# Second feed-forward of a two-layer backbone on one core: order of activations, of loads and of the last accumulation steps

## The reference

```python
def conv_ffn(h, w_up, conv_w, conv_b, w_down):
    T = h.shape[1]
    u = h @ w_up                                   # 1024 x 1024 @ 1024 x 5632
    up = jnp.pad(u, ((0, 0), (CONV_W // 2, CONV_W // 2), (0, 0)))
    u = sum(up[:, j:j + T] * conv_w[j] for j in range(CONV_W)) + conv_b
    gate, val = jnp.split(u, 2, axis=-1)           # 2816 each
    return (jax.nn.silu(gate) * val) @ w_down      # 2816 x 1024
...
    f = conv_ffn(modulate(x, mod[3], mod[4]), w_up[l], conv_w[l], conv_b[l], w_down[l])
    x = layer_norm(DEEPNORM_ALPHA * x + mod[5] * f, ln2_g[l], ln2_b[l])
```

## Time and profile before

| | us |
|---|---|
| median of 3 runs | 3586.43 (3586.16 to 3586.73) |
| the profiled execution | 3590.86, its span 3589.1 |
| TensorE busy in the span | 3399.7 (95%) |
| VectorE, ScalarE, GpSimd busy | 1741.4, 1194.6, 1188.3 |
| blocks 6 to 21 (seven products) | from 2993.2 to 3316.2 |
| down projection | from 3316.5 to 3577.1 |

### The profile page before, as it was taken

How to read it: one execution, slowest core, us unless ns; L and a number is a source line. 1 busy time by engine, 2 the same in 40 slices (tenths; PEclk the granted TensorE clock), 3 DMA queues, 4 the chain that set the end, 5 groups by cost and what they waited for, 6 DMA issues and landing times.

```text
span 3589.1 us, 57973 instructions
## 1 busy us (share of the span) xinstructions
PE 3399.7 (95%) x24535; PEld 2796.5 (78%) x24535; DVE 1741.4 (49%) x2789; ACT 1194.6 (33%) x1747; POOL 1188.3 (33%) x526
## 2 busy tenths in 40 slices
PE   7999999988999999999999899999979999999998
PEld 6777778877868888888887677788867678777787
DVE  4333563056177344433435743364067676555564
ACT  4334564124233111111113333365134334444332
POOL 1221101302233333333333311201303447888442
PEclk9999999999999999999999899999999999999999
DMA  5111001352201111111111101000162132222543
GB/s 195 32 23 30 1 2 48 100 182 55 72 24 41 36 41 36 36 42 36 36 42 71 29 23 29 24 2 19 36 201 66 53 118 62 79 74 89 202 157 113
DMA packets 288117, 229.46 MB, mean 64 GB/s; under 512 B 47068, under 2 KB 257908, under 8 KB 287860
## 3 DMA queue, kind: packets, MB, share of 16 engines
q1 hardware_dynamic: 286704, 225.28, 20.4%
q10 hardware_dynamic: 1156, 0.48, 0.0%
HBM read 201.60 MB, written 24.12 MB: 63 GB/s over the span
## 4 chain that ended last, share of the span: by engine, by line
PE 78%; POOL 8%; DVE 8%; issue 3%; ACT 2%; DMA 1%; SPq 1%; ACTq 0%; DVEq 0%; POOLq 0%
PE psum L1341 49%; PE psum L1132 6%; PE psum L1895 6%; PE psum L1447 5%; POOL up_op L1065 4%; PE psum L1605 3%; PE psum L1141 2%; PE psum L1533 2%; PE psum L1369 1%; POOL up_sums L1079 1%; DVE c_x L2594 1%; PE psum L1564 1%; PE psum L1689 1%; PE psum L1267 1%; DVE h_lo L2370 1%
## 5 line engine op out<-in xcount | busy, mean ns | idle before, releaser
L1341 PE MATMUL psum<-h_hi,w_split 128*128 128x512 f32 (+1 forms) x4992 | 1185.9, 367 | 20.8 <-DVEq L767 6.2
L1029 POOL TENSOR_SCALAR w_split<-w_raw 128x1024 fp32r<-128x1024 f32 x142 | 399.1, 2811 | 2067.6 <-PE psum L1341 1328.5
L1341 PEld LDWEIGHTS psum<-h_hi,w_split 128*128 128x128 f32 x4992 | 847.6, 188 | 195.3 <-issue 26.0
L1341 PE MATMUL psum<-h_lo,w_split 128*128 128x512 f32 (+1 forms) x2496 | 650.2, 364 | 0.0
L1341 PEld LDWEIGHTS psum<-h_lo,w_split 128*128 128x128 f32 x2496 | 424.7, 188 | 78.5
L2774 DVE SCALAR_TENSOR_TENSOR f_t<-psum,vec,f_t 128x1023 f32<-128x1023 f32 x194 | 170.3, 915 | 393.4 <-ACT f_t L3502 391.6
L1031 POOL TENSOR_TENSOR w_split<-w_raw,w_split 128x1024 fp32r<-128x1024 f32 x142 | 349.1, 2459 | 11.8
L3502 ACT ACTIVATE f_t<-psum,vec 128x1280 f32<-128x1280 f32 (+1 forms) x53 | 73.1, 1380 | 531.1 <-PE psum L1341 518.0
L1341 PE MATMUL psum<-f_hi,w_split 128*128 128x512 f32 (+1 forms) x1056 | 239.7, 357 | 1.5 <-DVE f_t L2774 1.5
L1341 PEld LDWEIGHTS psum<-f_hi,w_split 128*128 128x128 f32 x1056 | 176.2, 188 | 36.2 <-issue 5.7
L2630 DVE SCALAR_TENSOR_TENSOR y_chan<-psum,mods,y_chan 128x1024 f32<-128x1024 f32 (+1 forms) x176 | 146.3, 877 | 97.7 <-PE psum L1341 97.5
(11 more groups left out here) (360 smaller groups left out, 5389.0 us busy)
## 6 DMA issues: line engine op xcount, KB each, us to landing
ada_late<-in_w_ada_dram SPq DMA_DIRECT2D x32, 1024.0 KB, 7.0
w_raw<-in_w_up_dram SPq DMA_DIRECT2D x56, 512.0 KB, 3.8
w_raw<-in_w_in_dram SPq DMA_DIRECT2D x42, 512.0 KB, 3.8
w_raw<-in_w_down_dram SPq DMA_DIRECT2D x40, 512.0 KB, 3.7
up_raw<-in_w_up_dram SPq DMA_DIRECT2D x32, 512.0 KB, 5.3
f_raw<-f_mid SPq DMA_DIRECT2D x44, 256.0 KB, 3.9
l_raw<-in_w_down_dram SPq DMA_DIRECT2D x17, 512.0 KB, 3.6
ada<-in_w_ada_dram SPq DMA_DIRECT2D x4, 2048.0 KB, 16.5
```

The source lines that it names most:

```text
L1029: pool.tensor_scalar(w_hi[:, n % 2], w_raw[:, n % 2], 1.0, None, ALU.mult).then_inc(s["w_hi_done"], 1)
L1341: last = pe.matmul(columns(key, t0, t0 + tn), weight, a[:, k, t0:t0 + tn], start=(k == order[0] and j == 0), stop=(closes and k == order[- ...
```

## The change

1. Blocks 3 to 5. ScalarE's `begin(3, 0)` and `silu(3)`, and VectorE's `conv(3, 0)`, stand ahead of the first differences (VectorE's also ahead of the wait for `r_stored`). SyncE issues the weights of block 4's gate half after the fourth of the eight residual stores instead of behind the eighth.
2. The four low halves `h_lo` that GpSimd made in round 0 go to VectorE (`last_low_differences`).
3. Seven-product rounds. On ScalarE `begin(f - 1, 1)` and `silu(f - 1)` stand ahead of high operand 4. On GpSimd sum 2 stands behind low 1; low halves 0 and 1 count on `raw_ready`, the other five on `op_ready`.
4. Hand-over to the down projection. The homes of `w2` 1 and 2 change places; loads, and the splits into them, wait for the last product that reads the home instead of for all products; the eight reads of `y_back` are spread over steps 5 to 8 of the loads and the residual is added after step 8 instead of after step 4; the order of `gate_weights`, `low_tokens`, `conv(21, 1)`, `high_weights` changes.
5. `LAST_STEPS` = 2 becomes (2, 4): in the second group the last four steps run tile by tile.

```diff
-LAST_STEPS = 2
+LAST_STEPS = (2, 4)
...
-        w2 = [(h_raw[:, :, LAT + P:T], h_lo[:, :, LAT:LAT + P], h_lo[:, :, LAT + P:T]), in_w(1, pair_at), in_w(2, ring_at)]
+        w2 = [(h_raw[:, :, LAT + P:T], h_lo[:, :, LAT:LAT + P], h_lo[:, :, LAT + P:T]), in_w(1, ring_at), in_w(2, pair_at)]
...
                 def load_down(n):
-                    if n == 1:
-                        sp.wait_ge(s["op_ready"], 7 * N_FAST)
-                    elif 2 <= n < N_W2:
-                        sp.wait_ge(s["prod_done"], 7 * N_FAST)
+                    if n == 2:
+                        sp.wait_ge(s["op_ready"], 5 * N_FAST)
+                        sp.wait_ge(s["raw_ready"], 2 * N_FAST)
+                    elif 1 <= n < N_W2:
+                        sp.wait_ge(s["prod_done"], 7 * (N_FAST - 1) + 4)
...
                     elif n < N_F2:
-                        sp.wait_ge(s["prod_done"], 7 * N_FAST)
+                        sp.wait_ge(s["prod_done"], 7 * (N_FAST - 1) + 5)
...
                             sp.dma_start(r_mid[k], y_chan[:, k, 0:LAT]).then_inc(s["r_stored"], 16)
+                            if k == 3:
+                                weights_up_to("up", l, 4, 0)
...
                 for i in range(N_FAST):
+                    if i == N_FAST - 1:
+                        load_f(0)
+                        load_f(1)
                     store(fast_f + i - 1)
...
-                load_f(0)
-                load_f(1)
-                load_down(1)
-                load_f(2)
-                load_down(2)
+                for n in range(1, N_W2):
+                    load_down(n)
+                    if n > 1:
+                        load_f(n)
                 sp.wait_ge(s["r_stored"], 2 * 16 * KT)
-                for m in range(KT):
-                    sp.dma_start(y_back[:, m, 0:LAT], r_mid[m]).then_inc(s["y_back"], 16)
...
+                for n in range(N_W2, 2 * FT):
+                    if n < N_W2 + 4:
+                        for m in (2 * (n - N_W2), 2 * (n - N_W2) + 1):
+                            sp.dma_start(y_back[:, m, 0:LAT], r_mid[m]).then_inc(s["y_back"], 16)
...
                     pool.tensor_tensor(one, a21, a22, ALU.add).then_inc(s["sum_done"], 1)
-                    low(0, a11)
+                    for j, whole in enumerate((a11, a12)):
+                        n = 7 * i + j
+                        pool.wait_ge(s["op_hi"], n + 1)
+                        pool.tensor_tensor(up_ops[n % 4][:, 1], whole, up_ops[n % 4][:, 0].bitcast(F32), ALU.subtract)\
+                            .then_inc(s["raw_ready"], 1)
                     pool.wait_ge(s["sum_done"], 4 * i + 1)
                     pool.tensor_tensor(two, one, a11, ALU.subtract).then_inc(s["sum_done"], 1)
-                    low(1, a12)
                     pool.wait_ge(s["sum_done"], 4 * i + 2)
                     low(2, two)
...
-                    if i == 0:
-                        pool.wait_ge(s["t_ready"], 12)
-                        for k in range(4):
-                            pool.wait_ge(s["t_split_hi"], 13 + k)
-                            pool.tensor_tensor(h_lo[:, k, HALF:LAT], t_one[:, k], h_hi[:, k, HALF:LAT].bitcast(F32), ALU.subtract)\
-                                .then_inc(s["t_ready"], 1)
...
-                    if n == 1:
-                        pool.wait_ge(s["prod_done"], 7 * N_FAST)
+                    if n in (1, 2, 4):
+                        pool.wait_ge(s["prod_done"], 7 * N_FAST - (n != 2))
...
-                        if k == 4:
+                        if k == 8:
                             old_sums(group)
...
+                def last_low_differences():
+
+                    for k in range(4):
+                        dve.wait_ge(s["t_split_hi"], 13 + k)
+                        say("t_ready", dve.tensor_tensor(h_lo[:, k, HALF:LAT], t_one[:, k], h_hi[:, k, HALF:LAT].bitcast(F32),
+                                                         ALU.subtract))
...
                     gated(2)
+                    conv(3, 0)
                     dve.wait_ge(s["r_stored"], 2 * 16 * KT)
                     differences(0)
-                    conv(3, 0)
                     conv(3, 1)
...
                             if n == 1 and i == N_FAST - 1:
                                 low_tokens(0)
                                 low_tokens(1)
-                        if i == N_FAST - 1:
-                            gate_weights(1)
+                                gate_weights(1)
                         conv(f, 0)
-                    conv(FT - 1, 1)
                     gate_weights(2)
                     low_tokens(2)
+                    conv(FT - 1, 1)
                     gated(FT - 1)
...
-                    high_differences(0)
                     begin(3, 0)
                     silu(3)
+                    high_differences(0)
                     begin(3, 1)
...
                         take(i, 0)
-                        ahead(1)
                         if i:
                             begin(f - 1, 1)
                             silu(f - 1)
+                        ahead(1)
                         ahead(2)
                         take(i, 1)
...
                     begin(FT - 1, 1)
+                    high_tokens(2)
                     silu(FT - 1)
+                    high_weights(2)
```

More of the change, by code:

```diff
@@ L1907, in down_by_token @@
                 for group in range(2):
-                    for k in range(FT - LAST_STEPS):
+                    for k in range(FT - LAST_STEPS[group]):
                         n = FT * group + k
@@ L1924, in down_by_token @@
                     for i in range(4):
-                        for k in range(FT - LAST_STEPS, FT):
+                        for k in range(FT - LAST_STEPS[group], FT):
                             last = part(FT * group + k, i, False, k == FT - 1)
@@ L2875, in two_phases @@
                     differences(3)
-                    for half in range(2):
-                        conv(5, half)
+                    conv(5, 0)
+                    last_low_differences()
+                    conv(5, 1)
                     gated(5)
@@ L3442, in phase_post @@
             def phase_post():
-                for n in range(2, 2 * FT):
+                for n in range(3, 2 * FT):
                     if n == FT + 3:
@@ L3587, in two_phases @@
                     high_differences(3)
+                    begin(5, 0)
                     for n in range(3):
-                        if n == 2:
-                            begin(5, 0)
                         high_operand(n)
```

34 lines of the change are left out of this document (17 added, 17 removed).

## The result

The changed kernel takes 3566.91 us (median of 4 runs, 3562.34 to 3573.13), the kernel before 3586.58 in its runs beside it (4 runs, 3586.16 to 3589.08). The ratio is 0.9945, with a 95% interval of 0.9928 to 0.9962: the interval leaves 1 out, so the changed kernel is faster, by 19.7 us. The forecast was 3566.6.

What follows compares the result with a forecast made beforehand. The prediction took the loop of GpSimd and ScalarE, 20.22 us a round, as the bound. Terms 8.0 + 3.3 + 5.2 + 1.0 + 2.3 + 0 = 19.8 us took 3586.4 to 3566.6; range 3559 to 3576.

Steps and rivals of the forecast that it cites:

- Part 1, 8.0: Blocks 3 to 5: 5.1 for the wait in front of block 4 plus 2.9 for the clock; bounds 5 and 8.1.
- what would be late "next": Block 4's weight tile: with its load issued between residual stores, GpSimd's split starts near 2930 and ends six us early.
- the head start: Round 0: four low halves, 5.1 us of GpSimd, go to VectorE; 3.3 us gained, bounds 0 and 5.1.
- The timetable: GpSimd's seven-product round rebuilt instruction by instruction: from 20.22 to about 19.85 us, 5.2 us over fourteen rounds.
- the slower rival: Rounds: late gate taps make GpSimd, ScalarE and VectorE wait in a loop; 22.3 us a round, 3601 in all, chance 0.05.
- The join: Last round: TensorE's wait for `up_u` goes, as the product of the halves is done 1.7 us earlier; 1.0 us.
- The hand-over: First three down steps: 4.5 us of loss in place of 6.8, a gain of 2.3 us; bounds 0 and 6.
- the two counts of how late the tiles come: Hand-over to the down projection: third weight tile's chain 2.0 us late, the fourth 2.3 late again.
- Part 5, 0: Four last steps tile by tile: norms gain 4.3 us, a 3.4 wait and clock fall cost it; bounds -1 and +2.5.
- the middle between fall and no fall: Last four steps: +0.9 us with a clock fall of 1.8, -0.9 without; forecast took 0.
- The rivals: Rounds gain nothing 3572 (0.18); TensorE bounds rounds 3558 (0.10); block 4's wait moves 3575 (0.09); slower 3601 (0.05).
- The one in which TensorE bounds the rounds: Seven-product rounds: GpSimd and VectorE overlap better than the rows say, rounds of 19.1, 3558 us in all; chance 0.10.

Runs made afterwards that it cites:

- The load alone: Kernel before with only the weight load of block 4's gate half issued after the fourth residual store; 3585.83 us in one run, beside 3584.71 for the kernel before.
- the order alone: Kernel before with only begin, SiLU and taps of block 3's gate half ahead of the first differences; 3587.79 us in one run, beside 3584.71 before.
- the later table: Three kernels beside 11 runs of the kernel before (3588.32 us): sum 2 back with three last steps 3555.81, that plus third weight tile earlier 3556.61, changed 3566.42.

## Why the prediction was right, and where it was not

- **The bound.** The loop of GpSimd and ScalarE was the bound of a round and still is: TensorE waits 12 times on `up_op`, 0.43 to 0.48 us each. It is GpSimd's loop that sets 19.76 and 20.22, since taking out one wait of it, and nothing else, gives 19.04. TensorE became the bound only with sum 2 back in front.
- **Part 1, 8.0, measured 8.2.** The total was right. The step that failed is the attribution: I gave the whole wait to the place of the taps, and the load counted only as what would be late "next". The load alone is worth 4.7 in that stretch, since GpSimd's split no longer holds up the last differences, and the order alone 6.8; together they overlap.
- **Part 2, 3.3, measured 2.8.** The mechanism held; the head start was sized 0.5 too large.
- **Part 3, 19.85 a round, measured 19.76; 5.2 us, measured 6.2** (14 periods by 0.44). The timetable held piece by piece: the SiLU ends 11.62 us into the round (forecast 11.6), sum 4 at 13.91 (13.9), so the 2.3 us of room that spoke against the slower rival are there. The price of sum 2's place was exact in the timetable: sum 3 starts 7.28 into the round (forecast 7.28). Low 4 and low 5 together took 3.55 in place of some 3.7.
- **Part 4.** The join was 1.0 in the sum; of the 9.7 us of that stretch 2.8 and 6.2 are told, which leaves 0.7, the size of the wait that went. The hand-over was under-sized, 2.3 forecast and 3.6 measured. Three steps need 16.3 us and took 19.48: 3.2 of loss, where I left 4.5. The steps that failed are the two counts of how late the tiles come, 2.0 and 2.3, measured 1.00 and 1.69. That transfers held the first steps before is shown for step 3; for step 2 it was wrong, VectorE's taps stood in front of the gate there.
- **Part 5, 0, measured +1.9 in the first profile and +0.6 in the second.** The pieces were right (wait 3.4, measured 3.23; PE's end to the last norm 4.4, measured 4.3), and their sum with a clock fall was +0.9. The step that failed is taking the middle between fall and no fall. The clock fell in both: the last 96 matmuls need 21.9 us at full clock (96 by 2.72 / 12, and the last one's end) and took 24.8 and 23.5, so 2.9 and 1.6 where I had 1.8.
- **The rivals.** None came true in the changed kernel. The one in which TensorE bounds the rounds is what the code can do without sum 2's move.
- That forecast and result agree to 0.3 us is in part luck: errors of 1.3 and 1.9 us cancel, and the unchanged code alone varies by more than that. Beside the 11 runs of the later table the same change gave 21.9 us, not 19.7.

What stays open: the wait of 1.00 at step 2 goes when gate 2 stands ahead of the taps, and is 0.48 with sum 2 back in front; what share of it the slower splits have was not taken apart, nor were 2.6 of the 3.6 us of the hand-over.

## What to carry to other kernels

When one engine needs a result that a second engine makes from the first one's own last instruction (here low 2, which needs ScalarE's high half of sum 2), an independent instruction between the two hides the second engine's time. The SiLU's move helped by clearing ScalarE's way to such a result, worth 1.2 to 1.4 us a round; in the same change sum 2's move took the independent instruction away on GpSimd, and lost 0.7 to 0.9. So price each move of a change by itself, and run each alone before keeping all. Running last steps tile by tile buys back the work behind the matmuls only as long as the operands of all of them are there: a third step gave 4.1 us, a fourth cost 4.7 to 6.

## What was not expected of the hardware

- **The clock.** A granted clock between 0.50 and 1.00 is a mean over a stretch in which both levels, 1.2 and 2.4 GHz, occur. Behind TensorE's waits it did not follow the length of the wait alone. It stayed at 1.00 behind 1.69, 1.70 and, in front of block 4 with the early load, 3.18 us; in that same trace a second wait of 3.18, at down step 2, was followed by 0.50 over 5 us (first row). Behind the ten waits of 1.79 in the kernel with the SiLU in its old place it stayed at 1.00 seven times and was 0.66 over 5 us three times (second row). It was 0.66 for 5 us behind 1.91 too, and behind the 3.14 at step 2 of the kernel before, 0.67 behind 2.68, and 0.88 to 0.93 over 24 us behind 3.13 to 3.23. In a stretch that TensorE bounds the cost was 1.5 us after 1.91 and 2.9 after 3.23. So a wait of 2 to 3 us should be priced at up to twice its length, and with a range. Where another engine bounds the loop a fall cost nothing: behind the second row TensorE's next wait was 0.17 in place of 1.79 (third row), and the round stayed at 21.1.

```profile
3326.33:3331.33 5.00, 5.00 (x12) 3.94 (x13) 2.68 (x3) 2.21 (x3) 0.52 (x1) 0.50 1.03 409
```

```profile
3078.39:3083.39 5.00, 5.00 (x15) 3.95 (x16) 3.80 (x4) 1.83 (x4) 4.86 (x3) 0.66 0.25 92
...
3099.51 3.01 PE L1850 MATMUL psum<-t_part,up_op 128*128 128x512 f32 x12 [0.17 <-ACT taken L3006]
```

- **GpSimd's one-input split.** The product of block 2's halves (two SBUF inputs, VectorE, 2926.26) took 1.86 us beside `TENSOR_SCALAR` on GpSimd, which began 0.25 ahead and lasted 2.77; in the kernel with the order alone, with GpSimd at rest, the same product took 1.23. It ended before the GpSimd instruction, so it did not stand for the whole of it. The Trainium skill's page "SBUF — State Buffer" (section "Who interferes with whom") would have it stand until the other has finished; this row shows less. It reads the same in the second profile of the changed kernel (1.86 beside 2.77), and in the kernel before two differences with two SBUF inputs (at 2937.97, the row below, and at 2938.69) took their uncontended 0.69 us inside such an instruction (it lasted from 2935.85 to 2939.12 there). GpSimd's spans are rough in a profile, so this is a reading and no rule.

```profile
2937.97 0.69 DVE L2832 TENSOR_TENSOR taken<-taken,t_one 128x512 f32<-128x512 f32 x1
```
